# Zero matmuls in TensorE's longer waits of a hybrid decoder step on one core

## The chip, the cores and the metric

The kernel runs on one core of a Trainium2 chip. The metric is device time in microseconds (us) of one execution, and a kernel is told by the median of its runs. The engines are named as the profile names them: PE (TensorE: matmuls, and its weight loads as PEld), DVE (VectorE), ACT (ScalarE), POOL (GpSimd) and SP (the queue that issues most DMAs). TensorE's clock is granted at one of two levels, 1.2 and 2.4 GHz; the profile shows them as 0.50 and 1.00 of full speed.

## What is computed

One inference step of one layer: a prompt of 2048 tokens and 64 sample tokens, width 1024. In short:

```
mod = c @ w_ada + b_ada                       # sh1, sc1, g1, sh2, sc2, g2 for each sequence
u = x * (1 + sc1) + sh1
p, xr, gr = split(u @ w_in)                   # 1024 -> 3 x 512
y_pool = pool_mixer(p)                        # causal windows 2, 4, 8, 16, one 128x128 product for each group
xc = causal_conv(xr);  r, i = sigmoid(gates of xc);  h = scan(a(r), b(r, i, xc));  y_lru = h * gelu(gr)
x = LayerNorm(ALPHA * x + (1 + g1) * ([y_pool, y_lru] @ w_out))
u2 = x * (1 + sc2) + sh2
g_sel = argmax(u2 @ w_group);  top 2 of the 4 experts in that group, with weights   # 16 experts
y = sum over the two experts of w * (silu(u2 @ w_gate[e]) * (u2 @ w_up[e])) @ w_down[e]
x = LayerNorm(ALPHA * x + (1 + g2) * y)
```

The states of both mixers are outputs too.

## The kernel before

Every engine has its program written out by hand, and semaphores join them. PE works through its program strictly in the order of the text; nothing reorders it. Large products are made as three products of rounded halves (`split_product`, L1627, L1628 and L1629: high by high, high by low, low by high); small ones (gates L1648, pool groups L1657, router, counts) are plain f32 matmuls; transposes are matmuls with the identity `ident` (L1580).

PE's program, as far as the change touches it:

- **Start.** Transposes of the conditioning rows and states, the `ada` product, then the 64 sample rows times `w_in` (`sample_rows`, `turn_rows`). Then four waits on `proj_evac` and the split weights, and chunk 1.
- **Chunks.** `mixers(i)` does the 12 projections of a chunk of 256 tokens (24 products of 128x256 each), with gates and pool groups between them; there are 8 chunks. In chunk 1, after two projections, it calls `sample_mixers`: the 8 gate matmuls and 4 pool matmuls of the sample rows (64 columns). A pool group waits for DVE's difference `d_ready`, and DVE makes those of groups 2 and 3 only after the matmuls of groups 0 and 1. ACT copies the results, loads a table, takes roots, and only then evacuates chunk 1's first two projections, which projection 2 waits for.
- **Output projection.** `out_proj(t)` for 17 tiles, each two halves of 24 products of 512 columns; the first waits for the split weights and for `y_lo(0)` of DVE.
- **Routing.** After the last tile's router, PE counts the tokens of each expert (L1825, L1863) and waits for DVE's one-hot slots (`hot_ready`). Then 68 bf16 matmuls of 48 columns (L1870) give the token of every slot, DVE turns them into `tok_i` and the slots' experts, and POOL gathers the rows of the first slots by indirect DMA (`xg0`, `xg1`).
- **Slots.** 48 slots of 128 rows: `turn_x` transposes the gathered rows, ACT and DVE split them into halves, `gate_up` makes 24 products of 512 columns, ACT and DVE make the hidden rows, `turn_h` transposes them, `down` multiplies by `w_down`. From slot 1 on, `turn_x` and `down` of neighbouring slots stand between the parts of a slot; at slots 0 and 1 there is little to put between.
- The end is a sum with `ident_a` and `ident` in f32 (L1954, L1955) and the second LayerNorm.

`bank[5]` holds transposed states at the start, later the late `ada` sums of chunk 1 and on, the second half of `turn_u2`'s transposes, and in the slots the first half of `down`. `zero` is a 128x256 tile of zeros that POOL clears at the start.

Of the kernel before, what the change touches and what calls it, by code (L numbers as in the profile page):

```python
# [93 lines left out]
def build(nc, A):  # L94
    with ExitStack() as ctx:
        def sb(name, shape, dt=F32):
            return ctx.enter_context(nc.sbuf_tensor(name, shape, dt))
# [4 lines left out]
        bank = [ctx.enter_context(nc.psum_tensor(f"bank{n}", [P, 512], F32)) for n in range(8)]  # L102
# [132 lines left out]
        ident = sb("ident", [P, P])  # L235
# [33 lines left out]
        zero = sb("zero", [P, 256])  # L269
# [48 lines left out]
        def gate_bank(j, q):  # L318

            return q if j % 2 == 0 else 6 + q  # L320
# [1256 lines left out]
        def _(pe):  # L1577
            def turn(out, in_, rows):

                return pe.transpose(out, in_, ident[0:rows, 0:rows])  # L1580
# [12 lines left out]


            pe.wait_ge(S["cT_ok"], 1)

            def ada(k, g, w, start, stop):

                row = c_now[:] if k is None else cT[:, k, :]
                for j in range(4):  # L1600
                    last = pe.matmul(bank[(2, 4, 5)[g]][CW * j:CW * j + CW, :], row, w[:, DH * j:DH * j + DH], start=start, stop=stop)  # L1601
                return last
# [38 lines left out]
            def gates(i, groups, n, first=False):  # L1641
                for j in groups:
                    pe.wait_ge(S["xc_ready"], NG * i + j + 1)
                    for q, w in ((0, wa), (1, wx)):
                        if not (first and j < 2):

                            pe.wait_ge(S["gates_evac"], 2 * NG * i + 2 * j + q - 3)
                        pe.matmul(bank[gate_bank(j, q)][:, 0:n], w[:, j, :], xc[:, j, 0:n],  # L1648
                                  start=True, stop=True).then_inc(S["gates_mm"], 1)

            def pool_group(i, g, n, first=False):
                pe.wait_ge(S["d_ready"], NG * i + g + 1)
                if g == 0:
                    pe.wait_ge(S["gates_evac"], 2 * NG * i + 2 * NG)
                if not (first and g < 2):
                    pe.wait_ge(S["pool_evac"], NG * i + g - 1)
                pe.matmul(bank[6 + g % 2][:, 0:n], wp[:, g, :], dif[:, g % 2, 0:n], start=True, stop=True).then_inc(S["pool_mm"], 1)  # L1657
# [76 lines left out]
            def sample_mixers():  # L1734
                pe.wait_ge(S["gates_in"], 80)
                gates(0, range(NG), NS, first=True)
                for g in range(NG):
                    pool_group(0, g, NS, first=True)
                pe.wait_ge(S["gates_evac"], 2 * NG)

            pe.wait_ge(S["proj_evac"], 3 * NG)
            pe.wait_ge(S["win_hi"], 6)
            pe.wait_ge(S["win_lo_pool"], 3)
            pe.wait_ge(S["win_lo_dve"], 3)
            mixers(1, lambda: turn_chunk(2), sample=sample_mixers)
            with pe.Fori(2, NCH - 1) as i:
                mixers(i, lambda: turn_chunk(i + 1))
# [59 lines left out]
                pe.matmul(bank[6][0:n, P:P + NR], rt_sb[:, 0:n], pick[:], start=True, stop=True).then_inc(S["rt_mm"], 1)  # L1807

            pe.wait_ge(S["gates_evac"], 2 * NG * NCH + 2 * NG)
            pe.wait_ge(S["wout_lo_pool"], 4)  # L1810
            pe.wait_ge(S["wout_lo_dve"], 4)
            out_proj(0, 0, first=True)
# [49 lines left out]
            count(4)  # L1862
            pe.matmul(bank[1][:, 0:NE], ones[:], p_all[:, NT, :], start=True, stop=True).then_inc(S["cnt_mm"], 1)  # L1863

            for k in range(2):
                pe.wait_ge(S["hot_ready"], k + 1)
                pe.wait_ge(S["rows_ok2"], len(WEIGH))
                for t in range(NT):
                    for v, rows in enumerate((hot_t, hot_p)):
                        last = pe.matmul(bank[2][:, 0:SLOTS], rows[:, k, t, :], hot_s[:, k, t, :],  # L1870
                                         start=k + t + v == 0, stop=k == 1 and t == NT - 1 and v == 1)
            last.then_inc(S["idx_mm"], 1)


            pe.wait_ge(S["slots_ready"], 1)

            def turn_x(s, b, uses, first=False):
                pe.wait_ge(S[f"xg{b}"], 16 * uses)
                for h in range(2):
                    if not first:  # L1880
                        pe.wait_ge(S["xT_lo_ok"], 2 * s + h - 1)
                    for k in range(4):
                        last = turn(bank[h][:, k * P:(k + 1) * P], xg[b][:, (4 * h + k) * P:(4 * h + k + 1) * P], P)
                    last.then_inc(S["xgT_mm"], 1)

            def product(out, x_hi, x_lo, buf, off, start, stop):
                hi, lo = (w[:, ds(buf, 1), off:off + 512].rearrange("p a n -> p (a n)") for w in (w_hi, w_lo))
                return split_product(out, x_hi, x_lo, hi, lo, start, stop)

            def gate_up(s, b):  # L1890
                e = pe.value_load(slot_ei[0:1, 0, ds(s, 1)], min_val=0, max_val=NE - 1)
                pe.wait_ge(S["xT_lo_ok"], 2 * s + 2)

                pe.wait_ge(S["w_lo"], e * E_PARTS + GU_PARTS)
                for k in range(KD):
                    last = product(bank[2 + b][:, :], xT_hi[:, k, :], xT_lo[:, k, :], e & 1, k * 2 * F, k == 0, k == KD - 1)
                last.then_inc(S["gu_mm"], 1)

            def turn_h(s):
                pe.wait_ge(S["hid_ok"], s + 1)  # L1900
                for k in range(F // P):
                    last = turn(bank[4][:, k * P:(k + 1) * P], hid[:, k * P:(k + 1) * P], P)
                last.then_inc(S["hT_mm"], 1)

            def down(s, first=False):
                e = pe.value_load(slot_ei[0:1, 0, ds(s, 1)], min_val=0, max_val=NE - 1)
                pe.wait_ge(S["hT_lo_ok"], s + 1)
                pe.wait_ge(S["w_lo"], e * E_PARTS + E_PARTS)
                if not first:
                    pe.wait_ge(S["y_act"], s)  # L1910
                    pe.wait_ge(S["y_dve"], s)
                for h in range(2):
                    for k in range(F // P):
                        last = product(bank[5 + h][:, :], hT_hi[:, k, :], hT_lo[:, k, :], e & 1, GU + k * D + 512 * h,
                                       k == 0, k == F // P - 1)
                last.then_inc(S["dn_mm"], 1)

            turn_x(0, 0, 1, first=True)
            gate_up(0, 0)
            turn_x(1, 1, 1)  # L1920
            turn_h(0)
            for s in (1, 2):
                gate_up(s, s % 2)
                turn_x(s + 1, (s + 1) % 2, (s + 1) // 2 + 1)
                down(s - 1, first=s == 1)
                turn_h(s)
# [15 lines left out]
            for t in range(NT):  # L1942
                n = P if t < NT - 1 else NS
# [40 lines left out]
```

## Time and profile before

| | us |
|---|---|
| runs | 1276.79, 1272.21, 1277.30 |
| median of the runs | 1276.79 |
| the profiled execution | 1273.47 |
| its span, first to last instruction | 1271.4 |
| PE busy | 1160.1 |
| DVE busy | 868.3 |
| ACT busy | 551.3 |
| POOL busy | 308.0 |

The profile is of one execution, 1273.47 us, of which 2.1 us lie outside the span. Its mean granted clock is 0.956. Matmul ends are modelled, so the time of one matmul is read here from the starts of two that follow each other, and a stretch in which PE is busy throughout still goes at half the pace where the clock is 0.50.

### The profile page before, as it was taken

Reading aid. Unit: us, or ns where it says so; the run is one execution under the profiler, and the core shown is the slowest. Engines: PE = TensorE matmul, PEld = TensorE weight load, DVE = VectorE, ACT = ScalarE, POOL = GpSimd, SP = SyncE. Lnnn points to the kernel's source line nnn. Section 1 sums busy time; section 2 is a strip of 40 time slices with the busy share of each in tenths; the row PEclk is TensorE's granted clock in tenths of the full one; section 3 lists DMA queues with packets and bytes.
Section 4 is the critical chain, followed back from the end, with each engine's and each line's share of the span. In section 5 each row is a group of like instructions: output and inputs, shape, how many; then the busy total and the mean of one; then the engine's idle time right before and its main releaser. Section 6 shows DMA issues by size and latency. Waiting matters only on the chain.

```text
span 1271.4 us, 23320 instructions
## 1 busy us (share of the span) xinstructions
PE 1160.1 (91%) x6649; PEld 937.1 (74%) x6650; DVE 868.3 (68%) x1724; ACT 551.3 (43%) x1079; POOL 308.0 (24%) x431
## 2 busy tenths in 40 slices
PE   5889999999999489999997499999999999999495
PEld 2378988988989477787884478888888888888242
DVE  2774988988888688687888745566655654523298
ACT  0525336436435153343344344545545544422175
POOL 1411202202212230000000124444435534532100
PEclk9979999999999699999998599999999999999798
DMA  8914124214404264545343788779998889764773
GB/s 336 312 44 170 59 108 165 93 72 165 141 25 166 96 205 159 182 149 177 139 147 127 251 266 220 213 201 264 274 289 230 241 237 297 212 134 79 241 262 150
DMA packets 112897, 231.98 MB, mean 182 GB/s; under 512 B 11927, under 2 KB 70555, under 8 KB 109771
## 3 DMA queue, kind: packets, MB, share of 16 engines
q1 hardware_dynamic: 98947, 180.51, 40.8%
q0 software_dynamic: 13904, 50.87, 17.4%
q8 instruction: 27, 0.44, 0.1%
q14 instruction: 19, 0.16, 0.0%
HBM read 161.88 MB, written 70.11 MB: 182 GB/s over the span
## 4 chain that ended last, share of the span: by engine, by line
PE 78%; DVE 9%; issue 5%; ACT 4%; DMA 3%; SPq 1%; DVEq 0%; ACTq 0%
PE bank L1627 22%; PE bank L1629 21%; PE bank L1628 21%; PE bank L1580 6%; DMA ada_arena<-in_w_ada 2%; PE bank L1648 2%; PE bank L1715 2%; DVE ada_arena L1561 2%; PE bank L1601 2%; DVE arena L1168 1%; DVE ada_arena L1547 1%; PE bank L1657 1%; ACT arena L817 1%; PE bank L1802 1%; DVE arena L1149 0%
## 5 line engine op out<-in xcount | busy, mean ns | idle before, releaser
L1627 PE MATMUL bank<-parts 128*128 128x256 f32 (+2 forms) x1472 | 514.5, 350 | 31.7 <-ACT arena L767 20.9
L1629 PE MATMUL bank<-parts 128*128 128x256 f32 (+2 forms) x1472 | 496.9, 338 | 0.0
L1628 PE MATMUL bank<-parts 128*128 128x256 f32 (+2 forms) x1472 | 496.5, 337 | 0.0
L1627 PEld LDWEIGHTS bank<-parts 128*128 128x128 f32 x1472 | 282.9, 192 | 76.6 <-ACT arena L767 29.2
L1629 PEld LDWEIGHTS bank<-parts 128*128 128x128 f32 x1472 | 282.8, 192 | 28.5
L1628 PEld LDWEIGHTS bank<-parts 128*128 128x128 f32 x1472 | 283.7, 193 | 25.3
L1580 PE MATMUL bank<-ident,arena 128*128 128x128 f32 (+4 forms) x788 | 116.4, 279 | 19.0 <-DMA arena<-u_d,tok_i 5.8
L1580 PEld LDWEIGHTS bank<-ident,arena 128*128 128x128 f32 (+4 forms) x788 | 94.5, 146 | 44.7 <-issue 9.1
L1481 DVE TENSOR_TENSOR parts<-arena,parts x90 | 104.9, 1221 | 20.3 <-ACT parts L963 19.5
L1493 DVE TENSOR_TENSOR arena<-arena,bank 128x256 f32<-128x256 f32 x48 | 20.2, 421 | 132.5 <-ACT arena L976 132.1
L767 ACT ACTIVATE arena<-bank,proj_b 128x256 f32<-128x256 f32 x64 | 30.2, 473 | 146.0 <-PE bank L1629 146.0
L976 ACT ACTIVATE arena<-bank 128x256 f32<-128x256 f32 x48 | 18.5, 385 | 171.5 <-PE bank L1629 171.5
L650 POOL TENSOR_TENSOR arena<-arena 128x256 f32<-128x256 f32 (+1 forms) x36 | 26.1, 727 | 268.5 <-DVE h_last L1216 196.9
L963 ACT ACTIVATE parts<-arena x90 | 88.6, 1057 | 0.1
L702 POOL DMA_INDIRECT y_d<-arena,tok_out x48 | 83.5, 1740 | 16.2 <-issue 15.8
L1488 DVE TENSOR_TENSOR parts<-bank,parts 128x512 fp32r<-128x512 f32 x96 | 61.8, 685 | 24.1 <-ACT parts L971 24.1
L1627 PE MATMUL bank<-parts,y_arena 128*128 128x512 f32 (+1 forms) x144 | 59.3, 412 | 3.9 <-DVE y_arena L1156 3.9
L699 POOL COPY tok_out<-tok_i 128x1 int32 (+1 forms) x48 | 13.9, 290 | 196.1 <-DMA y_d<-arena,tok_out 150.1
L1168 DVE RECIPROCAL arena<-arena 128x256 f32<-128x256 f32 (+1 forms) x36 | 58.3, 1620 | 1.2
L987 ACT ACTIVATE arena<-bank,wslot 128x512 f32<-128x512 f32 x48 | 33.1, 689 | 59.9 <-PE bank L1629 59.9
L1505 DVE TENSOR_SCALAR arena<-bank,wslot 128x512 f32<-128x512 f32 x48 | 36.0, 749 | 33.7 <-PE bank L1629 33.7
L1628 PE MATMUL bank<-parts,y_arena 128*128 128x512 f32 (+1 forms) x144 | 56.9, 395 | 0.0
(263 smaller groups left out, 1671.6 us busy)
## 6 DMA issues: line engine op xcount, KB each, us to landing
arena<-in_w_ada SPq DMA_DIRECT2D x16, 1024.0 KB, 8.4
arena<-in_w_gate SPq DMA_DIRECT2D x16, 1024.0 KB, 7.3
arena<-in_w_up SPq DMA_DIRECT2D x16, 1024.0 KB, 13.5
arena<-in_w_down SPq DMA_DIRECT2D x16, 1024.0 KB, 15.3
y_d<-zero SPq DMA_DIRECT2D x17, 512.0 KB, 6.4
ada_arena<-in_w_ada SPq DMA_DIRECT2D x4, 2048.0 KB, 15.1
arena<-in_x_prompt SPq DMA_DIRECT2D x8, 1024.0 KB, 7.2
yT_d<-arena SPq DMA_DIRECT2D x16, 512.0 KB, 4.6
```

Of the source, the lines that this page charges most:

```text
L702: pool.indirect_dma_start(out=y_d, out_offset=bass.IndirectOffsetOnAxis(ap=tok_out[b][:, 0:1], axis=0), in_=y_sb[b], in_offset=None, compu ...
L767: act.activation(dst, bank[2 + m % 2][:, 0:C], ACT.Identity, bias=proj_b[:, m:m + 1]).then_inc(S["proj_evac"], 1)
L963: act.activation(part(w_hi, e & 1, n), raw_part(e & 1, n), ACT.Copy).then_inc(S["w_hi"], 1)
L987: act.activation(y_sb[b][:, 0:512], bank[5][:, :], ACT.Copy, scale=wslot[:, ds(s, 1)]).then_inc(S["y_act"], 1)
L1168: o.step(dve.reciprocal(q_t[:, 0:n], q_t[:, 0:n]))
L1481: dve.tensor_tensor(part(w_lo, e & 1, n), raw_part(e & 1, n), part(w_hi, e & 1, n).bitcast(F32), ALU.subtract).then_inc(S["w_lo"], 1)
L1488: dve.tensor_tensor(xT_lo[:, k, :], bank[h][:, :].rearrange("p (k n) -> p k n", n=P), xT_hi[:, k, :].bitcast(F32), ALU.subtract).then_inc( ...
L1505: dve.tensor_scalar(y_sb[b][:, 512:1024], bank[6][:, :], wslot[:, ds(s, 1)], None, ALU.mult).then_inc(S["y_dve"], 1)
L1580: return pe.transpose(out, in_, ident[0:rows, 0:rows])
L1627: pe.matmul(out, x_hi, w_hi, start=start, stop=False)
L1628: pe.matmul(out, x_hi, w_lo, start=False, stop=False)
L1629: return pe.matmul(out, x_lo, w_hi, start=False, stop=stop)
```

## The change

A function `keep_busy(n)` is added to PE's program: n matmuls of the 128x128 identity by the 128x256 tile of zeros, f32, into the first 256 columns of `bank[5]`. It is called in ten lines of the text, in all for 98 matmuls: 9 before chunk 1; in `sample_mixers` 3 after the gates, 3 after each of the four pool groups and 7 more after the last; 11 before the first output projection; 18 before the slot matmuls of routing and 22 behind them; 6 after slot 0's `turn_x`, 4 after slot 1's, and 6 after slot 0's `turn_h`. Nothing waits for them and they write nothing that is read. Two waits come with them: on `zero_ok` at the start and on `mod_ok` before the 11. The other engines' programs are unchanged.

```diff
             pe.wait_ge(S["cT_ok"], 1)
+            pe.wait_ge(S["zero_ok"], 2)
+
+            def keep_busy(n):
+
+                for _ in range(n):
+                    pe.matmul(bank[5][:, 0:256], ident[:], zero[:], start=True, stop=True)
...
             def sample_mixers():
                 pe.wait_ge(S["gates_in"], 80)
                 gates(0, range(NG), NS, first=True)
+                keep_busy(3)
                 for g in range(NG):
                     pool_group(0, g, NS, first=True)
+                    keep_busy(3)
+                keep_busy(7)
                 pe.wait_ge(S["gates_evac"], 2 * NG)
 
+            keep_busy(9)
             pe.wait_ge(S["proj_evac"], 3 * NG)
...
             pe.wait_ge(S["gates_evac"], 2 * NG * NCH + 2 * NG)
+            pe.wait_ge(S["mod_ok"], 2)
+            keep_busy(11)
             pe.wait_ge(S["wout_lo_pool"], 4)
...
+            keep_busy(18)
             for k in range(2):
                 pe.wait_ge(S["hot_ready"], k + 1)
...
             last.then_inc(S["idx_mm"], 1)
-
+            keep_busy(22)
 
             pe.wait_ge(S["slots_ready"], 1)
...
             turn_x(0, 0, 1, first=True)
+            keep_busy(6)
             gate_up(0, 0)
             turn_x(1, 1, 1)
+            keep_busy(4)
             turn_h(0)
+            keep_busy(6)
             for s in (1, 2):
```

PE's program in the sample stage of chunk 1, before: the sample gates and pool groups (64 columns, L1648 and L1657), then the next projection.

```order
L1648 MATMUL bank<-arena 128x64 [waits gates_evac]
L1657 MATMUL bank<-arena 128x64 [waits gates_evac,d_ready]
L1657 MATMUL bank<-arena 128x64 [waits d_ready]
L1657 MATMUL bank<-arena 128x64 [waits pool_evac,d_ready] x2
L1627 MATMUL bank<-parts 128x256 [waits proj_evac,gates_evac]
```

The same place in the changed program, where line numbers are larger (L1654, L1663 and L1633 are the three lines above) and L1601 is the zero matmul:

```order
L1654 MATMUL bank<-arena 128x64 [waits gates_evac]
L1601 MATMUL bank<-zero,ident 128x256 x3
L1663 MATMUL bank<-arena 128x64 [waits gates_evac,d_ready]
L1601 MATMUL bank<-zero,ident 128x256 x3
L1663 MATMUL bank<-arena 128x64 [waits d_ready]
L1601 MATMUL bank<-zero,ident 128x256 x3
L1663 MATMUL bank<-arena 128x64 [waits pool_evac,d_ready]
L1601 MATMUL bank<-zero,ident 128x256 x3
L1663 MATMUL bank<-arena 128x64 [waits pool_evac,d_ready]
L1601 MATMUL bank<-zero,ident 128x256 x10
L1633 MATMUL bank<-parts 128x256 [waits proj_evac,gates_evac]
```

Nothing changed its order; zero matmuls stand between all four pool groups and ahead of the projection, and none of them waits.

PE's program from the slot matmuls of routing to slot 0, before (L1870 the slot matmuls, L1580 `turn_x`, then slot 0's `gate_up`):

```order
L1870 MATMUL bank<-ada_arena 128x48 [waits rows_ok2,hot_ready]
L1870 MATMUL bank<-ada_arena 128x48 x33
L1580 MATMUL bank<-ident,arena 128x128 [waits xg0,slots_ready]
L1580 MATMUL bank<-ident,arena 128x128 x7
L1891 TENSOR_LOAD slot_ei
L1894 ISA [waits xT_lo_ok]
L1627 REGISTER_ALU [waits w_lo]
```

And in the changed program:

```order
L1601 MATMUL bank<-zero,ident 128x256 x18
L1883 MATMUL bank<-ada_arena 128x48 [waits rows_ok2,hot_ready]
L1883 MATMUL bank<-ada_arena 128x48 x33
L1601 MATMUL bank<-zero,ident 128x256 x22
L1580 MATMUL bank<-ident,arena 128x128 [waits xg0,slots_ready]
L1580 MATMUL bank<-ident,arena 128x128 x7
L1601 MATMUL bank<-zero,ident 128x256 x6
L1904 TENSOR_LOAD slot_ei
L1907 ISA [waits xT_lo_ok]
```

Again the order of the rest is kept: 18, 22 and 6 zero matmuls stand ahead of three waits.

## Rows read from the trace of the kernel before

**Rows 1.** The page: clock in 40 slices; the chain that ended last, by engine.

```profile
PEclk9979999999999699999998599999999999999798
...
PE 78%; DVE 9%; issue 5%; ACT 4%; DMA 3%; SPq 1%; DVEq 0%; ACTq 0%
```

**Rows 2.** PE's waits: line, releaser, us in total, times, longest.

```profile
PE bank L1627 <- ACT arena L767: 20.9, 2, 18.1
```

**Rows 3.** Stretches: length, busy us (matmuls) of PE, PEld, DVE, ACT, POOL; clock; DMA; GB/s.

```profile
63.37:66.78 3.41, 3.41 (x18) 3.41 (x17) 3.06 (x13) 0.00 (x0) 0.00 (x0) 0.50 0.02 5
...
78.84:83.84 5.00, 5.00 (x23) 5.00 (x24) 4.52 (x19) 0.23 (x1) 0.00 (x0) 0.50 0.42 161
461.10:464.28 3.18, 0.06 (x2) 0.03 (x1) 3.03 (x3) 2.03 (x4) 0.00 (x0) 1.00 0.75 274
...
723.37:728.97 5.60, 5.60 (x13) 4.49 (x14) 1.92 (x2) 0.13 (x1) 0.00 (x0) 0.50 1.07 376
...
735.79:739.20 3.41, 3.41 (x9) 2.66 (x9) 3.41 (x4) 2.36 (x3) 0.00 (x0) 0.50 1.07 383
739.20:1150.00 410.80, 410.69 (x2022) 341.07 (x2022) 224.15 (x308) 191.30 (x350) 178.79 (x263) 1.00 0.83 233
```

**Rows 4.** PE's timeline, first chunk: start, us, line, out<-in, shape, records; idle before, releaser.

```profile
58.92 0.47 PE L1580 MATMUL bank<-ident,arena 65*128 65x65 f32 x4 [0.44 <-ACT arena L839]
61.87 0.35 PE L1627 MATMUL bank<-parts 128*128 128x256 f32 x1 [2.48 <-ACT arena L861]
...
69.07 0.28 PE L1629 MATMUL bank<-parts 128*128 128x256 f32 x1
69.19 1.45 PE L1648 MATMUL bank<-arena 128*128 128x64 f32 x12
...
72.86 0.63 PE L1657 MATMUL bank<-arena 128*128 128x64 f32 x4 [1.33 <-ACT arena L817]
...
75.29 0.69 PE L1657 MATMUL bank<-arena 128*128 128x64 f32 x2 [0.87 <-DVE arena L1239]
78.84 0.55 PE L1627 MATMUL bank<-parts 128*128 128x256 f32 x1 [2.86 <-ACT arena L767]
```

**Rows 5.** The chain at 443 us: start, us, line, records of f32 128x256.

```profile
442.90 1.73 PE bank L1648 x8
```

**Rows 6.** PE's timeline where the final sum begins (f32 with 128x512).

```profile
1195.14 2.04 PE L1954 MATMUL bank<-arena 128*128 128x512 f32 x2 [14.96 <-issue]
1196.97 1.92 PE L1955 MATMUL bank<-ada_arena,ident 128*128 128x512 f32 x2
1198.68 1.68 PE L1954 MATMUL bank<-arena 128*128 128x512 f32 x2
1200.20 1.02 PE L1955 MATMUL bank<-ada_arena,ident 128*128 128x512 f32 x2
```

**Rows 7.** PE's timeline at the first output projections.

```profile
460.13 1.02 PE L1657 MATMUL bank<-arena 128*128 128x256 f32 x4
464.28 0.47 PE L1627 MATMUL bank<-parts,y_arena 128*128 128x512 f32 x1 [3.12 <-DVE y_arena L1156]
...
487.40 0.50 PE L1627 MATMUL bank<-parts,y_arena 128*128 128x512 f32 x1 [0.79 <-DVE y_arena L1156]
```

**Rows 8.** PE's timeline from the last count to slot 1.

```profile
702.56 0.59 PE L1863 MATMUL bank<-ada_arena,ones 128*128 128x16 f32 x2
710.94 2.90 PE L1870 MATMUL bank<-ada_arena 128*128 128x48 bf16 x68 [7.79 <-DVE ada_arena L1446]
719.63 1.94 PE L1580 MATMUL bank<-ident,arena 128*128 128x128 f32 x8 [5.79 <-DMA arena<-u_d,tok_i]
723.37 0.79 PE L1627 MATMUL bank<-parts 128*128 x1 [1.80 <-DVE parts L1488]
...
731.57 1.53 PE L1580 MATMUL bank<-ident,arena 128*128 128x128 f32 x10
735.05 0.49 PE L1627 MATMUL bank<-parts 128*128 x1 [1.96 <-DVE parts L1488]
```

## The prediction, made before the changed kernel was run

> **What bounds the kernel now.** I read the page first, for the clock and for the chain that ended last [rows 1]. The chain is PE for 78% of the span, so what delays PE mostly delays the end. The clock is full nearly everywhere; its low slices are at the first chunk, at the last chunk, in routing and at the end. Then PE's waits: the largest by far, 18.1 us for ACT's L767 in the last chunk [rows 2], gets no zero matmuls and stays. Then the stretches in which PE works without pause at clock 0.50 [rows 3]: 63.37 to 66.78 us, 78.84 to 83.84, 723.37 to 728.97, 735.79 to 739.20. These 17.4 us are what the change can win back, about half of their length. From 739.20 to 1150.00 PE is busy for 410.69 of 410.80 us [rows 3]: whatever comes later or earlier at slot 1 reaches the end whole.
>
> **Price of one zero matmul.** The trace has the same shape in the gates: f32, 128x128 by 128x256, two records each. Eight records take 1.73 us [rows 5], so a matmul costs 0.43 us at full clock. At half clock I double it, 0.86: the f32 matmuls of 512 columns at the end start 1.71 us apart, two records each [rows 6], which is 0.85 for 256 columns. All 98 cost 42 us at full clock. Each group is compared with the wait that it stands in, since what is longer than its wait makes PE late.
>
> **First wait (9).** PE's transposes end at 59.39 and chunk 1 starts at 61.87 after 2.48 us of waiting [rows 4]. Nine cost 3.90, so chunk 1 starts at 63.29: 1.4 us late. In return the clock should not fall at 63.37. The pace there is 0.12 us a product at full clock (69.07 to 69.19 [rows 4]) and 0.217 at half (23 in 5.00 us [rows 3]), so a stretch at half clock loses 45% of its length: 3.41 us lose 1.5. Net −0.1.
>
> **Sample stage (22).** Three after the gates fit in the 1.33 us ahead of the first pool group [rows 4]. Then three (1.30 us) plus a pool group of about 0.25 three times over take 4.65 us; before, the last group followed the first after 2.43 us (72.86 to 75.29 [rows 4]). That is +2.2, and DVE and ACT, who wait for the groups, come later too. Behind the last group stand ten, 4.33 plus 0.25 us, where 3.55 us passed before (75.29 to 78.84 [rows 4]): +1.0. So projection 2 starts 3.2 us later than it would. Its low stretch of 5.00 us [rows 3] loses 2.2 less. Net +1.0; the first chunk together +0.9. The 18.1 us wait later on does not hide this as far as I can see, since the DVE and ACT work that ends it is itself fed by PE's projections; if it does hide it, the sum is 0.9 smaller.
>
> **First output projection (11).** The last pool groups' four records start at 460.13 and at 0.217 each end at 461.0; eleven cost 4.76, to 465.8, where the projection started at 464.28 [rows 7]: 1.5 late. The clock did not fall in this wait (1.00 from 461.10 to 464.28 [rows 3], and no low slice behind it), so nothing is won back in this execution. Tile 2's wait of 0.79 us for DVE [rows 7] takes up part. Net +0.7. In an execution whose clock does fall here, the zero matmuls would save some 1.5 and the net would be about −0.8.
>
> **Routing (18).** They start at about 703.15, behind the last count, with the clock still low, and the wait is 7.79 us [rows 8]: exactly 18 at full clock. But the clock needs time. In the end stage it was full 4.9 us after dense f32 work began (1195.14 to about 1200.1 [rows 6]); elsewhere 5.0 (78.84 to 83.84) and 5.6 (723.37 to 728.97) [rows 3]. In 4.9 us at 0.86 go 5.7 matmuls, the other 12.3 take 5.3 us: end at 713.4, 2.4 us after the slot matmuls could start. These took 2.90 us at low clock [rows 8]; at full clock between half and all of it, and I take half: −1.45. Net +0.95 (bounds +0.9 and +2.4). DVE's `tok_i` and POOL's gather wait for it.
>
> **First slots (22, 6, 4, 6).** Between the slot matmuls and `turn_x` lay 5.79 us [rows 8]; 22 cost 9.53: +3.7. From `turn_x` to `gate_up` there were 3.74 us (719.63 to 723.37 [rows 8]); now 0.9 us of transposes at full clock and 2.6 of zeros, about 3.5: −0.2. `gate_up` of slot 0 took 8.2 us (723.37 to 731.57 [rows 8]) for 24 products, 5.6 us of it at low clock; at the 0.23 us of full clock it takes 5.5: −2.7. Then 731.57 to 735.05 was 3.48 us [rows 8]; now eight transposes 0.9, zeros 1.7, two transposes 0.25, zeros 2.6, together 5.45: +2.0. The hidden rows are ready before the four are done, so `turn_h` is late by PE alone, and `down` behind it is not reached yet. The low stretch 735.79 to 739.20 [rows 3] held 8 or 9 products of 0.43 us, 0.2 more than at full clock: −1.6. Net of the slots +1.2. Weight loads on SP's queue do not wait for any of this.
>
> **Sum.** 0.9 + 0.7 + 0.95 + 1.2 = 3.75 us later: the overruns add up to some 13.5 us, the clock gives back about 9.7. Against the profiled execution's 1273.47 us that is 1277.2. That execution lies 3.3 us under the median of the runs, 1276.79; runs from 1272.2 to 1277.3 show how far executions of one program lie apart, and a reason is visible: the clock fell after a wait of 2.48 us and held through one of 3.12 us [rows 3, 4], so it is partly chance where it falls. The mean of the three runs and the profiled one is 1275.0; with 3.75 it gives 1278.7. I forecast **1279 us**, which is 0.2% above the median of before. A difference below 0.5%, 6.4 us, can't be told from none here.
>
> **Rivals.**
> - **The clock is not won back (slower).** The overruns are sure, since PE works in order and the zeros wait for nothing; the gains rest on a clock that stays up. If it falls between the groups, or in routing rises so late that `gate_up` still starts low, the loss stays and the gain goes. With none of 9.7 us won the time is 1279 + 9.7, about 1288. The point is where about 5 of the 9.7 come back: below that the result is over 1283.2, slower by more than 0.5%. For it: the first-slot gains (2.7 + 1.6) need the clock up through routing, where it had been low since 688, and executions whose clock fell less before have less to win. Against: dense f32 work with the identity did raise the clock [rows 6]. Should zeros not count as work at all, so that the groups in the sample stage and routing go at 0.86, it would be some 25 us worse still; I hold that for 2 in 100. Chance in all 0.23.
> - **Short zeros (faster).** If a zero matmul cost one pass of 0.12 us, like a product of the same columns at L1627 [rows 4], 98 would take 12 us, no group would outlast its wait, and the price would be nothing; they would also fill only a third of the waits. Between none and all of the 9.7 us would be won; half gives 1275 − 5 = 1270. Against it stand the gate rows [rows 5], of the same type and shape. The Trainium skill, "TensorE: Matmul & The Clock Gate", section "Back-to-back issue gap", gives the gap by columns and clock alone, with no word on the type; for 256 columns its formula is an estimate of 0.11 us, and the sum by it would be this rival's. The gate rows, at 0.43, disagree for f32. Chance 0.05.
> - **The delays are hidden (same or a little faster).** If the 18.1 us wait of the last chunk [rows 2] takes up the first chunk's 0.9, and other executions do lose clock at the output projection, so that its +0.7 turns to −0.8, the sum is 3.75 − 2.4 = 1.35 and the time about 1276; with more luck in the clock before, below 1272. Chance 0.10, of it 0.03 faster than 0.5%.
>
> **How the numbers follow.** The forecast has 0.62. Same: 0.62 of the forecast and 0.07 of the hidden delays, 0.69. Slower: 0.23. Faster: 0.05 and 0.03, 0.08. The range reaches down to 1271, where all terms at their low ends and the short zeros meet, and up to 1287, where nearly nothing of the clock is won.
>
> **What will show it.** In the changed kernel's trace: zero matmuls at 0.43 us apart at full clock (0.12 would speak for short zeros); clock 1.00 from chunk 1's start through its sample stage, with projection 2 starting about 3 us later in the stage than before but ending less than 1.5 us later; the first output projection starting right behind its zeros, not at DVE's release; in routing, a clock that rises some 5 us into the 18, slot matmuls of about 1.5 us, and `gate_up` of slot 0 at 5.5 us in place of 8.2; PE without a wait where each group stands. The prediction fails if groups end before their waits do, if the clock is 0.50 in `gate_up` of slot 0 or 1, or if PE waits in chunk 1 for ACT or DVE longer than I allow.

## The result, and the profile of the changed kernel

The changed kernel takes 1277.57 us (median of 22 runs, 1274.91 to 1283.33). The kernel before, run beside it, takes 1273.49 us (22 runs, 1271.24 to 1277.3). The ratio is 1.0032, with a 95% interval of 1.0021 to 1.0044: some 4.1 us slower, real but below the 0.5% bound of the forecast. The profiled execution took 1275.9 us with a span of 1273.8, against 1273.47 and 1271.4 before.

The page of the changed kernel, clock in 40 slices and the chain that ended last by engine, for comparison with [rows 1]:

```profile
PEclk9999999999999799999998899999999999999798
...
PE 81%; DVE 6%; issue 4%; ACT 3%; SPq 3%; DMA 2%; POOL 1%; ACTq 0%; DVEq 0%
```

The low slice at the first chunk is gone and the one in routing is milder. PE's share of the chain grew from 78% to 81%: PE now works where it used to wait. The lines have moved: products are L1633 to L1635 (L1627 to L1629 before), gates L1654, pool groups L1663, slot matmuls L1883, and the zero matmuls are L1601.

Stretches of the changed kernel (length; busy us and records of PE; clock; DMA; GB/s): from chunk 1's start to projection 2, behind it, the 18 zeros of routing, and `gate_up` of slots 0 and 1:

```profile
62.75:81.50 18.75, 18.48 (x119) 1.00 0.19 65
81.50:86.50 5.00, 5.00 (x43) 1.00 0.02 5
704.68:713.87 9.19, 9.19 (x37) 0.85 0.88 284
728.44:734.11 5.67, 5.67 (x27) 1.00 1.04 385
739.33:745.01 5.68, 5.68 (x27) 1.00 0.67 263
```

Four of these hold the work that ran at 0.50 in [rows 3]. Now it runs at 1.00; only the zeros of routing start low.

PE's timeline of the changed kernel in the first chunk, for [rows 4] (start, us, line, out<-in, shape, records; idle before and releaser; one f32 matmul leaves two records):

```profile
58.70 0.46 PE L1580 MATMUL bank<-ident,arena 65*128 65x65 f32 x4 [0.44 <-ACT arena L839]
59.00 4.10 PE L1601 MATMUL bank<-zero,ident 128*128 128x256 f32 x18
62.75 0.47 PE L1633 MATMUL bank<-parts 128*128 128x256 f32 x1
...
68.68 1.45 PE L1654 MATMUL bank<-arena 128*128 128x64 f32 x12
...
72.37 0.41 PE L1663 MATMUL bank<-arena 128*128 128x64 f32 x2
...
77.16 4.54 PE L1601 MATMUL bank<-zero,ident 128*128 128x256 f32 x20
81.35 0.47 PE L1633 MATMUL bank<-parts 128*128 128x256 f32 x1
...
93.14 1.06 PE L1607 MATMUL bank<-arena,cT 128*32 128x512 f32 x8
```

No row behind a group of zeros has a wait in brackets: PE no longer waits there, and what was a wait is now filled to its end or past it. The three behind the gates just fit: the first pool group starts 3.69 us behind the first gates (68.68 to 72.37), where it started 3.67 behind them before [rows 4]. The ten behind the last pool group take 77.16 to 81.35, 0.42 us each.

The same at the first output projection, for [rows 7], and from the last count to the end of slot 1's `gate_up`, for [rows 8]:

```profile
458.48 0.39 PE L1633 MATMUL bank<-parts 128*128 128x256 f32 x1 [2.10 <-ACT arena L776]
461.46 1.02 PE L1663 MATMUL bank<-arena 128*128 128x256 f32 x4
462.32 4.91 PE L1601 MATMUL bank<-zero,ident 128*128 128x256 f32 x22
466.88 0.58 PE L1633 MATMUL bank<-parts,y_arena 128*128 128x512 f32 x1
...
489.18 0.40 PE L1633 MATMUL bank<-parts,y_arena 128*128 128x512 f32 x1
```

```profile
704.26 0.59 PE L1875 MATMUL bank<-ada_arena,ones 128*128 128x16 f32 x2
704.68 9.35 PE L1601 MATMUL bank<-zero,ident 128*128 128x256 f32 x36
713.87 1.87 PE L1883 MATMUL bank<-ada_arena 128*128 128x48 bf16 x68
715.59 9.74 PE L1601 MATMUL bank<-zero,ident 128*128 128x256 f32 x44
725.16 1.04 PE L1580 MATMUL bank<-ident,arena 128*128 128x128 f32 x8
...
728.44 0.58 PE L1633 MATMUL bank<-parts 128*128 x1
734.11 1.04 PE L1580 MATMUL bank<-ident,arena 128*128 128x128 f32 x8
...
739.33 0.58 PE L1633 MATMUL bank<-parts 128*128 x1
745.01 1.04 PE L1580 MATMUL bank<-ident,arena 128*128 128x128 f32 x8
```

Two rows of the kernel before close the same stretches there (start, us, line):

```profile
92.72 1.07 PE L1601 MATMUL bank<-arena,cT 128*32 128x512 f32 x8
...
742.21 1.04 PE L1580 MATMUL bank<-ident,arena 128*128 128x128 f32 x8
```

The rows at 93.14 and 92.72 are the `ada` product behind the sixth of chunk 1's twelve projections. So from the last transposes ahead of chunk 1 to the middle of that chunk the changed kernel spends 34.44 us (58.70 to 93.14), where 33.80 went before (58.92 to 92.72), and 40.75 us (704.26 to 745.01) from the last count to the end of slot 1's `gate_up`, where 39.65 went (702.56 to 742.21): +0.64 and +1.10. "The first chunk" below means the first of these two stretches.

### The profile page after: what moved, and what is told of

The parts are those of the page before. It is cut to its first block, busy times and chain, and to the rows that moved or that the text cites. A ratio compares the mean times of both kernels' runs of the same rounds, so it can differ in the third digit from the quotient of the medians.

```text
span 1273.8 us, 23712 instructions
## 1 busy us (share of the span) xinstructions
PE 1191.2 (94%) x6845; PEld 965.0 (76%) x6846; DVE 866.9 (68%) x1724; ACT 552.0 (43%) x1079; POOL 312.9 (25%) x431
## 4 chain that ended last, share of the span: by engine, by line
PE 81%; DVE 6%; issue 4%; ACT 3%; SPq 3%; DMA 2%; POOL 1%; ACTq 0%; DVEq 0%
PE bank L1633 22%; PE bank L1635 21%; PE bank L1634 21%; PE bank L1580 6%; PE bank L1601 3%; DVE ada_arena L1561 2%; PE bank L1654 2%; PE bank L1607 1%; PE bank L1721 1%; DVE ada_arena L1547 1%; SPq L372 1%; PE bank L1663 1%; SPq L343 1%; POOL parts L667 1%; PE bank L1812 1%
## 5 line engine op out<-in xcount | busy, mean ns | idle before, releaser
L1633 PE MATMUL bank<-parts 128*128 128x256 f32 (+2 forms) x1472 | 510.7, 347 | 24.3 <-ACT arena L767 17.9
L1635 PE MATMUL bank<-parts 128*128 128x256 f32 (+2 forms) x1472 | 493.5, 335 | 0.0
L1633 PEld LDWEIGHTS bank<-parts 128*128 128x128 f32 x1472 | 279.9, 190 | 67.9 <-ACT arena L767 29.0
L1635 PEld LDWEIGHTS bank<-parts 128*128 128x128 f32 x1472 | 279.6, 190 | 28.1
L1634 PEld LDWEIGHTS bank<-parts 128*128 128x128 f32 x1472 | 280.3, 190 | 25.0
L1580 PE MATMUL bank<-ident,arena 128*128 128x128 f32 (+4 forms) x788 | 115.5, 277 | 13.4 <-DVE arena L1313 5.1
L1580 PEld LDWEIGHTS bank<-ident,arena 128*128 128x128 f32 (+4 forms) x788 | 94.0, 145 | 38.7 <-DVE parts L1127 7.1
L699 POOL COPY tok_out<-tok_i 128x1 int32 (+1 forms) x48 | 17.0, 355 | 197.0 <-DMA y_d<-arena,tok_out 158.8
L1633 PE MATMUL bank<-parts,y_arena 128*128 128x512 f32 (+1 forms) x144 | 59.3, 412 | 0.0
## 6 DMA issues: line engine op xcount, KB each, us to landing
arena<-in_w_up SPq DMA_DIRECT2D x16, 1024.0 KB, 13.5
```

The source lines that it names most:

```text
L1633: pe.matmul(out, x_hi, w_hi, start=start, stop=False)
L1634: pe.matmul(out, x_hi, w_lo, start=False, stop=False)
L1635: return pe.matmul(out, x_lo, w_hi, start=False, stop=stop)
```

## Experiments

Two questions were open. Does the small loss come from two large amounts that nearly cancel, overruns of some 13.5 us against some 9.7 us of clock, or from two small ones? And does each overrun reach the end, or does a later wait take it up?

**One place at a time.** Three kernels keep the zero matmuls of one place each and drop the rest.

```
 e1_first_chunk:       keep_busy(9), keep_busy(3), 4 x keep_busy(3), keep_busy(7)
 e2_output_projection: keep_busy(11)
 e3_routing_slots:     keep_busy(18), keep_busy(22), keep_busy(6), keep_busy(4), keep_busy(6)
```

> Only the 31 zero matmuls of the first chunk are left (9 ahead of it, 22 in the sample stage). Length against wait (my theory: a group costs what it is longer than its wait, less the low clock that it removes): clock 1.00 from 59 us on, projection 2 about 3 us later than before against the start of chunk 1's wait, and 0.4 to 0.9 us lost by the end of chunk 1, so about 1274.2 against 1273.5 of before. Hidden delays: the 18 us wait of the last chunk takes it up, no difference from before or a little faster. Clock not won back: 4.6 us slower, about 1278.

> Only the 11 zero matmuls ahead of the first output projection are left. Length against wait: the projection starts 1.5 us or more late, tile 2's wait for DVE of 0.8 us takes up part; 0.7 to 1.7 us slower than before, about 1274.7. If in most executions of before the clock does fall behind this wait, it is about 0.8 us faster than before, 1272.7. Clock not won back says the same as the first, so this run only sizes the term.

> Only the 56 zero matmuls of routing and the first slots are left (18, 22, 6, 4, 6). Length against wait: slot matmuls start 1.2 to 2.4 us late and take 1.7 to 1.9 us in place of 2.9, turn_x starts some 5 us late, gate_up of slots 0 and 1 take 5.7 us each in place of 8.2 and 7.2; slot 1's end is 1.1 to 2.2 us later than before counted from the last count, so about 1275.1. Clock not won back: the overruns alone, 8 us slower, 1281.

Beside 1273.41 us of before: the first chunk alone 1274.93 (ratio 1.0009, 0.9996 to 1.0023), the output projection alone 1273.12 (0.9996, 0.9983 to 1.0009), routing and slots alone 1274.84 (1.0016, 1.0003 to 1.003). Every place is small by itself, and none shows the loss of a clock that is not won back: the interval ends at 2.9 us for the first chunk and at 3.8 us for routing and slots, where 4.6 and 8 were expected for that. The ratios add up to some 2.7 us where the whole change has 4.1; with about 1.7 us of uncertainty on each that is no contradiction, but the timings alone can't rank the places. The first chunk's profile repeats the changed kernel's: 34.44 us again (59.32 to 93.76). In the output projection's profile the last pool groups start at 462.19 and tile 2 at 489.91, 27.72 us apart, as in the changed kernel (461.46 to 489.18) and 0.45 more than before (460.13 to 487.40 in [rows 7]). The projection's +0.45 shows twice in the traces, and its timing neither confirms nor contradicts so little. Routing and slots come out otherwise than in the changed kernel:

```profile
703.07 0.59 PE L1870 MATMUL bank<-ada_arena,ones 128*128 128x16 f32 x2
703.50 10.70 PE L1601 MATMUL bank<-zero,ident 128*128 128x256 f32 x36
714.03 1.87 PE L1878 MATMUL bank<-ada_arena 128*128 128x48 bf16 x68
...
745.17 1.03 PE L1580 MATMUL bank<-ident,arena 128*128 128x128 f32 x8
```

From the last count to the end of slot 1's `gate_up` it is 42.10 us (703.07 to 745.17), +2.45 against before, a little over the expected 2.2 and more than twice the changed kernel's +1.10. All of the difference lies in the 18 zeros, which take 10.53 us here and 9.19 there.

**Zeros of half the width.** All 98 stay, over half the columns.

```diff
-                    pe.matmul(bank[5][:, 0:256], ident[:], zero[:], start=True, stop=True)
+                    pe.matmul(bank[5][:, 0:128], ident[:], zero[:, 0:128], start=True, stop=True)
```

> All 98 zero matmuls stay where they are, each over 128 columns instead of 256; what the kernel computes is unchanged. Length against wait (the forecast's theory): the price goes by the columns, 0.217 us at full clock, 98 = 21 us. Then 9 take 1.95 us in a wait of 2.48, the sample stage's groups of three with a pool group 0.9 us each (at most 0.3 us over), ten 2.2 us in 3.55, 11 take 2.4 us in 3.12, 22 take 4.8 us in 5.79: no group outlasts its wait by more than 0.3 us, and between half and nearly all of the 9.7 us of clock is won: 1264.5 to 1268, about 1266. Clock not won back: no overrun and no gain, about 1273. Price by the instruction (0.43 us each whatever the columns): as the changed kernel, 1277.6.

Measured: 1264.72 us beside 1274.08, ratio 0.9924 (0.9907 to 0.994). PE's timeline of this kernel:

```profile
59.17 2.23 PE L1601 MATMUL bank<-zero,ident 128*128 128x128 f32 x18
61.83 0.36 PE L1633 MATMUL bank<-parts 128*128 128x256 f32 x1 [0.43 <-ACT arena L861]
...
460.07 2.62 PE L1601 MATMUL bank<-zero,ident 128*128 128x128 f32 x22
462.44 0.48 PE L1633 MATMUL bank<-parts,y_arena 128*128 128x512 f32 x1
...
710.05 5.16 PE L1601 MATMUL bank<-zero,ident 128*128 128x128 f32 x44
716.57 1.07 PE L1580 MATMUL bank<-ident,arena 128*128 128x128 f32 x8 [1.35 <-DMA arena<-u_d,tok_i]
```

The zeros stand in twelve groups, counting what stands together as one. Six of them now end before their wait does (9, 3 behind the gates, 10, 18, 22, and 6 behind slot 0's `turn_x`), and waits of 0.4 to 1.7 us are back behind them. Behind the other six PE doesn't wait, but they cost little: the three groups between the pool groups make the last pool group 0.3 us late, the others next to nothing. What is left is nearly all gain. The first chunk takes 30.10 us (58.87 to 88.97), 3.70 less than before; the forecast had put its two clock gains at 1.5 and 2.2. Count to slot 1 takes 34.52 (699.89 to 734.41), 5.13 less. With the same number of instructions the kernel went from 0.3% slower to 0.8% faster, so the loss lies in the length of the zeros and not in their count, and the price by the instruction (1277.6) falls. Eleven zeros of 128 columns take 2.37 us (460.07 to 462.44), 0.22 each, where eleven of 256 took 4.56 in the changed kernel (462.32 to 466.88).

**Counts fitted to the waits.** The width stays 256, and the groups get as many as fit: 60 zeros in all. In the order of the program: behind the pool groups, first wait, output projection, routing, first slots.

```diff
-                    keep_busy(3)
-                keep_busy(7)
+                    keep_busy((0, 0, 2, 6)[g])
-            keep_busy(9)
+            keep_busy(5)
-            keep_busy(11)
+            keep_busy(7)
-            keep_busy(18)
+            keep_busy(13)
-            keep_busy(22)
+            keep_busy(13)
-            keep_busy(4)
-            keep_busy(6)
+            keep_busy(5)
```

> All ten places, but each group cut to the length of its wait at 0.43 us a matmul: 5 ahead of chunk 1; 3, 0, 0, 2 and 6 in the sample stage; 7 ahead of the output projection; 13 and 13 around the slot matmuls; 6, 0 and 5 in the slots (60 in place of 98). Length against wait: no PE delay above 0.5 us at any group, and nearly all of the 9.7 us of low clock still won: about 1265, 8 to 9 us faster than before. Clock not won back: the clock falls again in or behind the shorter groups, and the time is that of before, 1273, or at most 2 us below it.

Measured: 1265.47 us beside 1273.41, ratio 0.9939 (0.9922 to 0.9956). PE's timeline of it:

```profile
59.27 2.38 PE L1601 MATMUL bank<-zero,ident 128*128 128x256 f32 x10
61.91 0.35 PE L1633 MATMUL bank<-parts 128*128 128x256 f32 x1 [0.27 <-ACT arena L861]
...
74.12 2.81 PE L1601 MATMUL bank<-zero,ident 128*128 128x256 f32 x12
77.14 0.36 PE L1633 MATMUL bank<-parts 128*128 128x256 f32 x1 [0.21 <-ACT arena L767]
```

The remaining waits are 0.2 to 0.3 us here and at most 0.55 elsewhere; one group, the 13 of routing, still makes what follows late, by 0.4 us. The first chunk takes 29.86 us (58.96 to 88.82). Fewer zeros or shorter ones come to the same within the intervals, and both beat both kernels. That no zero matmul is needed behind the first and the second pool group, where PE waits 0.3 us at most, is a side result: the clock is 1.00 throughout the first chunk.

A gain of the first chunk doesn't arrive whole, though. In the half-width profile that chunk is 3.70 us shorter than before, but tile 2 of the output projection starts only 2.68 earlier (484.72 against 487.40); in the fitted one it is 3.94 shorter, and tile 2 starts 2.29 earlier (485.11), behind a wait of 2.19 us for DVE's L1156 that was 0.79 before [rows 7].

**Twice as many.** Every count doubled, 196 in all (`keep_busy(3)` becomes `keep_busy(6)`, and so on).

> Every group of zero matmuls has twice the count, 196 in all; what the kernel computes is unchanged. Length against wait: in the changed kernel every group already outlasts its wait and the clock is already won, so the added 98 stand on the path whole: 98 x 0.43 = 42 us over the changed kernel, about 1320 (1318 to 1321). Hidden delays: if the 17.9 us wait of the last chunk takes up what the first chunk is late, the 31 zeros added there (13.4 us) don't reach the end, and about 1306 comes out. Clock not won back (part of the added zeros at half clock, 0.86 us): 1325 or more.

Measured: 1318.48 us beside 1274.08, ratio 1.035 (1.0333 to 1.0368), 40.9 us over the changed kernel: 0.42 us for each added zero. PE's wait in the last chunk in this kernel, and in the changed one (line, releaser, us in total, times, longest):

```profile
PE bank L1633 <- ACT arena L767: 18.0, 1, 18.0
```

```profile
PE bank L1633 <- ACT arena L767: 17.9, 1, 17.9
```

The first chunk now takes 47.60 us (58.48 to 106.08), 13.16 more than in the changed kernel, and the wait of the last chunk is as long as it was. So it takes up nothing: what ends it is as late as PE is. That settles the rival in which the delays are hidden, which the timing of the first chunk alone (0.9996 to 1.0023) could not.

**More waits filled.** On top of the half-width kernel, three groups in waits that the change leaves alone, each into a bank that is unused there: 74 in the last chunk's wait of 18.3 us, 20 in one of 5.1 us in routing, 60 in one of 15.4 us ahead of the final sums.

```diff
+                if order == 6:
+                    keep_busy(74, 7)
...
+            keep_busy(20)
             turn_u2(NT - 2, 1)
...
+            keep_busy(60, 0)
             pe.wait_ge(S["ident_a_ok"], 1)
```

> The half-width kernel (98 zero matmuls of 128 columns) with three more groups, all shorter than their waits by its trace at 0.235 us each: 74 (17.4 us) into an unused bank in the 18.3 us wait of the last chunk, 20 (4.7 us) in the 5.1 us wait ahead of routing's last but one transposes, 60 (14.1 us) in the 15.4 us wait ahead of the final sums; what the kernel computes is unchanged. Length against wait: the low stretch behind each wait shortens, 434.37 to 438.3 by 1.8 us, the final sums' 1188.3 to 1193 by some 2.2, routing's transposes and router by up to 1.5 (less if the short waits behind them let the clock fall again): 3 to 5.5 us under the half-width kernel, 1259 to 1262, ratio to before about 0.989. Hidden gains: if what follows those waits waits for ACT or DVE anyway, little of it reaches the end, and 1263 to 1266 comes out, ratio 0.992 to 0.994.

Measured: 1262.74 us beside 1273.07, ratio 0.9914 (0.9895 to 0.9933). Against 0.9924 (0.9907 to 0.994) that is no difference that these runs can resolve, and it lies between the two expectations. Rows of the half-width kernel at the three places, and then of this one:

```profile
434.37 0.58 PE L1633 MATMUL bank<-parts 128*128 128x256 f32 x1 [18.30 <-ACT arena L767]
454.75 0.39 PE L1633 MATMUL bank<-parts 128*128 128x256 f32 x1 [1.78 <-ACT arena L776]
...
686.77 1.97 PE L1580 MATMUL bank<-ident,arena 128*128 128x128 f32 x8 [5.09 <-DVE arena L1313]
690.77 1.08 PE L1812 MATMUL bank<-arena,w_rt 128*32 128x128 f32 x16 [2.03 <-ACT arena L882]
...
1188.31 2.05 PE L1970 MATMUL bank<-arena 128*128 128x512 f32 x2 [15.38 <-issue]
...
1193.13 1.02 PE L1971 MATMUL bank<-ada_arena,ident 128*128 128x512 f32 x2
```

```profile
433.64 0.39 PE L1633 MATMUL bank<-parts 128*128 128x256 f32 x1 [1.77 <-ACT arena L767]
453.34 0.39 PE L1633 MATMUL bank<-parts 128*128 128x256 f32 x1 [2.85 <-ACT arena L776]
...
685.39 1.09 PE L1580 MATMUL bank<-ident,arena 128*128 128x128 f32 x8 [0.53 <-DVE arena L1313]
689.39 1.05 PE L1814 MATMUL bank<-arena,w_rt 128*32 128x128 f32 x16 [2.91 <-ACT arena L882]
...
1185.77 1.10 PE L1974 MATMUL bank<-arena 128*128 128x512 f32 x2 [1.75 <-issue]
...
1188.42 1.02 PE L1975 MATMUL bank<-ada_arena,ident 128*128 128x512 f32 x2
```

All three waits are filled, and the work behind each starts at full clock. In routing it is worth nothing: the transposes take 1.09 instead of 1.97 us, and the wait for ACT's L882 behind them grows from 2.03 to 2.91, by the same 0.88, since ACT's copies start with the first transposes. In the last chunk the next wait for L776 grew by 1.07 us; whether the earlier work made it longer is open, since without this group its longest lies anywhere from 0.2 to 2.1 us from kernel to kernel. Ahead of the final sums the full gain arrives: from the first of them to the fourth 2.65 us instead of 4.82. Within one profile each the hidden gain in routing and the 2.17 us at the end are clear; their sum is too small for the medians.

## Why the prediction was right, step by step

**Price.** Forecast 0.43 us a zero matmul from the gate rows [rows 5]; measured 0.42 in the changed kernel and in the doubled one. The short zeros (0.12 us) are ruled out. The Trainium skill, "TensorE: Matmul & The Clock Gate", section "Back-to-back issue gap", gives the gap by columns and clock alone; its formula is an estimate of 0.11 us for 256 columns and 0.056 for 128. The traces have 0.42 and 0.22 for f32, nearly four times as much at both widths.

**First chunk.** The first wait ends 1.10 us later than before (4.05 us from the transposes to chunk 1 against 2.95; forecast 1.4). From chunk 1's start to projection 2 it takes 18.60 us against 16.97, +1.63; forecast were 3.2 of overrun less 1.5 of clock, +1.7. The first gates part the two: up to them 5.93 us against 7.32, −1.39 of clock; from there 12.67 against 9.65, +3.02 of overrun. From projection 2 to the `ada` product behind the sixth projection 11.79 us against 13.88, −2.09; forecast −2.2. Net +0.64 against +0.9, and it stays through the last chunk's wait, as the forecast took it and the doubled kernel shows.

**First output projection.** From the last pool groups the projection starts 5.42 us later instead of 4.15: +1.27 (forecast +1.5). The whole shift at tile 2 is 1.78 us, but 1.33 of it is there already when the pool groups start, from a wait of 2.10 us for L776 that was 0.5 before. The zeros' own part at tile 2 is +0.45 against +0.7. The term was right in kind and a little too large. The longer wait is not the zeros' doing as far as the profiles show: ACT's L800, which stands ahead of that L776, waited 3.31 us for a DMA in this execution and 1.73 before, and PE's wait is 0.8 us with the output projection's zeros alone and 0.7 with the first chunk's.

**Routing.** In the changed kernel's profile this term was mis-sized. The 18 zeros took 9.19 us, the slot matmuls start 9.61 us behind the last count against 8.38, +1.23; forecast +2.4. The forecast took 4.9 us until the clock is full; here it was full 2.7 us after the first zero, by 707.4, while in the kernel with routing and slots alone it took 5.4 us, until 708.9, the zeros took 10.5 us, and the slot matmuls were 2.6 us late, close to the forecast's 2.4. So the forecast had one possible value of a time that varies. The 68 slot matmuls took 1.72 us (713.87 to 715.59) against 2.90, −1.18; forecast −1.45. Net +0.05 against +0.95 (+1.40 in the kernel with routing and slots alone).

**First slots.** The 22: 9.57 us against 5.79, +3.78 (forecast +3.7). `turn_x` to `gate_up`: 3.28 against 3.74, −0.46 (−0.2). `gate_up` of slot 0: 5.67 against 8.20, −2.53 (−2.7). To slot 1: 5.22 against 3.48, +1.74 (+2.0). `gate_up` of slot 1: 5.68 against 7.16, −1.48 (−1.6). Net +1.05 against +1.2.

**The sum.** The zeros' net parts in the profiles are 0.64 + 0.45 + 0.05 + 1.05 = 2.2 us, against 3.75 forecast and +4.1 (2.7 to 5.6) by the medians. The profiled pair is 2.4 us apart. Behind the 2.2 stand two large amounts, as forecast: by the stretches above the overruns make 11.3 us and the clock gives back 9.1, where the forecast had 13.5 and 9.7. The experiments give the same picture by the medians. By the half-width kernel the clock is worth 9.7 us (7.6 to 11.8 by its ratio's interval). The changed kernel lies 13 to 14 us over it (12.9 by the two medians, 13.8 by the ratios), which is what the overruns cost. So the mechanism holds in size, not only in sign. That the sum of 3.75 comes so near to +4.1 is in part luck: with the +2.45 that routing and slots alone show for that stretch, in place of 1.10, the parts add up to 3.5. One profile a kernel can't say which of the two is the rule, and stretches that hold no zeros differ from profile to profile as well (with the first chunk alone by 1.6 us between 800 and 900 us, where PE has waits of 0.8 and 0.5 us that it doesn't have before). So the 1 to 2 us between the profiled sum and the medians stay unexplained.

**The level.** The forecast of 1279 us began at 1275.0, the mean of the three runs and the profiled one. Over 22 runs before lies at 1273.49, and with the same 3.75 that is 1277.2. So the forecast of 1279 lies over the measured 1277.57 mostly because its starting level was 1.5 us too high.

**The rivals.** The clock was won back: no fall between 59 and 420 us in the changed kernel, and 1.00 in both `gate_up`. With none of it won the half-width kernel would have stayed at about 1273. Short zeros and hidden delays fell with the prices and the last chunk's wait above.

## What to carry to other kernels

Fill a wait of TensorE only up to its length: filler that ended within its waits, or within a few tenths of a microsecond of them, made this kernel 0.6 to 0.8% faster, and the same filler at twice the length made it 0.3% slower, because past the end of a wait each filler matmul costs its full time. Take the price of a filler matmul from a row of its type and shape (f32 of 256 columns took 0.42 us, a product of rounded halves of the same columns 0.12), and leave a few tenths of a microsecond of the wait over. What a filled wait returns is at most about half of the stretch at low clock behind it, and nothing where the next wait is for another engine's work that starts no sooner.

## What the runs showed of the hardware

- Matmuls of zeros kept the clock at 1.00 (62.75 to 86.50 us, where it had fallen twice before) and raised it from 0.50 in routing: in these runs zeros counted as work like the products.
- How soon the clock rises differs for the same instructions: 2.7 us after the first zero of routing in the changed kernel, 5.4 us with the same 18 zeros in another kernel.
- From the length of a short wait alone the fall of the clock can't be told here: it held through waits of 2.10 us (458.48 in the changed kernel) and 3.12 us [rows 7], and fell within 1.5 us behind waits of 1.78 us (454.75 in the half-width kernel, 0.50 from 455.4 to 458.8) and 2.48 us [rows 3, 4].
- An f32 zero matmul of 256 columns takes 0.42 us and one of 128 takes 0.22, where a product of rounded halves of 256 columns takes 0.12.
